# Seven block products for eight in the second feed-forward product of an encoder step, its weight remainders made by accumulating transfers

## The reference

```python
h = _rmsnorm(x, g_mix); p = h @ w_in                  # 1024 -> 7168
x = x + (sigmoid(g_conv)*conv_branch + sigmoid(g_attn)*attention) @ w_out
def _mlp(x, g, w_up, w_down):
    h = _rmsnorm(x, g)
    return jnp.square(jax.nn.relu(h @ w_up)) @ w_down # 1024 -> 4096 -> 1024
x = x + _mlp(x, g_mlp, w_up, w_down)                  # then a final RMSNorm
```

## Time and profile before

| | |
|---|---|
| median of 3 runs | 952.39 us |
| the profiled execution | 951.78 us, of which the traced span is 950.0 us |
| PE busy | 940.7 us, 99% |
| DVE, ACT, POOL busy | 535.8 us, 527.2 us, 257.2 us |
| DMA | 111.37 MB, mean 117 GB/s |

### The profile page before, as it was taken

The page is one execution under the profiler, slowest core; times in us unless marked ns, Lnnn a source line. Parts: engine busy times, 40 slices in busy tenths (PEclk is TensorE's granted clock), DMA queues, the critical chain, the costliest instruction groups (busy, mean ns, idle before and its releaser), DMA issues.

```text
span 950.0 us, 19721 instructions
## 1 busy us (share of the span) xinstructions
PE 940.7 (99%) x7473; PEld 922.4 (97%) x7473; DVE 535.8 (56%) x917; ACT 527.2 (55%) x824; POOL 257.2 (27%) x188
## 2 busy tenths in 40 slices
PE   8999999999999999999999999999999999999997
PEld 8999999999999999999999999999999999999997
DVE  6579999999999999996753332221111122221133
ACT  6788888878787878786733343333111133331153
POOL 5311110101010101012243444445333244454340
PEclk9999999999999999999999999999999999999999
DMA  6777676766767585668132223233323133243102
GB/s 181 163 170 144 154 145 156 133 169 125 176 120 181 112 188 105 148 154 203 45 110 89 83 76 108 87 90 112 89 89 89 47 89 88 88 122 97 45 23 95
DMA packets 189520, 111.37 MB, mean 117 GB/s; under 512 B 35437, under 2 KB 181277, under 8 KB 189482
## 3 DMA queue, kind: packets, MB, share of 16 engines
q1 hardware_dynamic: 176666, 80.28, 30.7%
q0 software_dynamic: 7632, 27.79, 16.1%
q10 hardware_dynamic: 5184, 2.78, 1.1%
HBM read 75.97 MB, written 7.06 MB: 87 GB/s over the span
## 4 chain that ended last, share of the span: by engine, by line
PE 95%; ACT 1%; DMA 1%; POOL 1%; DVE 1%; issue 0%; ACTq 0%; DVEq 0%
PE dense L551 81%; PE z L671 3%; PE dense L846 3%; PE z L635 2%; PE z L705 2%; POOL w_lo L516 1%; PE z L551 1%; DMA w_lo<-w_raw 1%; PE z L639 1%; DMA x_tok<-in_x_sample_dram 1%; PE dense L715 0%; ACT n L957 0%; PE z L838 0%; PE z L629 0%; PE z L691 0%; PE z L710 0%
## 5 line engine op out<-in xcount | busy, mean ns | idle before, releaser
L534 POOL TENSOR_TENSOR w_lo<-w_raw,w_hi 128x1024 fp32r<-128x1024 f32 x80 | 192.3, 2408 | 294.9 <-ACT w_hi L939 294.9
L551 PE MATMUL dense<-r_hi,w_hi 128*128 128x272 f32 (+1 forms) x1264 | 263.5, 291 | 1.2 <-DMA w_lo<-w_raw 0.7
L551 PE MATMUL dense<-r_lo,w_hi 128*128 128x272 f32 (+1 forms) x1264 | 262.7, 289 | 0.0
L551 PE MATMUL dense<-r_hi,w_lo 128*128 128x272 f32 (+1 forms) x1264 | 262.3, 289 | 0.0
L939 ACT ACTIVATE w_hi<-w_raw 128x1024 fp32r<-128x1024 f32 x134 | 140.7, 1052 | 115.4 <-PE dense L551 102.7
L551 PEld LDWEIGHTS dense<-r_hi,w_hi 128*128 128x128 f32 x1264 | 198.2, 188 | 1.6 <-DMA w_lo<-w_raw 0.8
L551 PEld LDWEIGHTS dense<-r_lo,w_hi 128*128 128x128 f32 x1264 | 198.8, 188 | 0.7 <-DVE r_lo L1352 0.6
L551 PEld LDWEIGHTS dense<-r_hi,w_lo 128*128 128x128 f32 x1264 | 199.2, 188 | 0.0
L1371 DVE SCALAR_TENSOR_TENSOR acc<-conv_in,cw_cur,acc 128x574 f32<-128x574 f32 x232 | 172.8, 809 | 0.5
L511 POOL DMA_DIRECT2D w_lo<-w_raw x53 | 45.1, 851 | 361.2 <-ACT w_lo L941 361.2
L551 PE MATMUL dense<-s_hi,w_hi 128*128 128x272 f32 x640 | 132.2, 288 | 0.0
(11 more groups left out here) (258 smaller groups left out, 1287.0 us busy)
## 6 DMA issues: line engine op xcount, KB each, us to landing
w_raw<-in_w_in_dram SPq DMA_DIRECT2D x54, 512.0 KB, 6.0
w_lo<-w_raw POOLq DMA_DIRECT2D x53, 512.0 KB, 5.0
w_raw<-in_w_up_dram SPq DMA_DIRECT2D x32, 512.0 KB, 4.0
w_raw<-in_w_down_dram SPq DMA_DIRECT2D x32, 512.0 KB, 3.5
w_raw<-in_w_pw_dram SPq DMA_DIRECT2D x8, 512.0 KB, 3.6
w_raw<-in_w_out_dram SPq DMA_DIRECT2D x8, 512.0 KB, 3.5
x_tok<-in_x_prompt_dram SPq DMA_DIRECT2D x4, 512.0 KB, 6.1
out_dram<-k_blk SPq DMA_DIRECT2D x32, 64.0 KB, 2.4
```

Source lines behind the costliest of these rows:

```text
L534: pool.tensor_tensor(w_lo[:, n], w_raw[:, n], w_hi[:, n].bitcast(F32), ALU.subtract).then_inc(lo_post, 1)
L551: mm = nc.tensor.matmul(out[:, h, 0:half], w[:, wslot, k, :], m[:, k, c0 + h * half:c0 + (h + 1) * half], start=(k == 0 and n == 0), stop= ...
```

## The change

Three of four rounds of the down product are done as a 2 x 2 block product with seven products for eight (Strassen's method in Winograd's form). A round covers 8 feature blocks. For each of its four pairs of output tiles (`P_`, 12 in all), A is the pair's weights, divided into even and odd output tile and even and odd feature block; B is the activations, divided into even and odd feature block and first and second 272 tokens. PE makes seven products (`SEVEN`), each of 4 blocks x 3 passes = 12 matmuls of 272 columns. DVE adds them to `xT` in nine additions from PSUM (`add_product`).

The forms of A are A11, A12, A22 and four sums S1 to S4, each 128 x 512. DVE makes the four sums (`wsum_pair`, into part of `gate_c`); ACT writes the rounded form into `w_hi` and the rounded negated form into `w_lo`; POOL then issues one accumulating transfer of 256 KB for each form. The forms of B (four quarters, of which three are used as they are, and T1 to T4, DVE's) are made in `up`. The feed-forward part now runs as four rounds of 8 up tiles, each followed by its part of the down product; the fourth is as before.

```diff
+        BY_DMA = ('A11', 'S1', 'A12', 'S2', 'S4', 'S3', 'A22')
+        SEVEN = (("A11", "B11", 0, True), ("S1", "T1", 1, True), ("A12", "B21", 2, True), ("S2", "T2", 0, False),
+                 ("S4", "B22", 3, True), ("S3", "T3", 0, False), ("A22", "T4", 2, True))
+        def quarter(P_, name):
+            slot = 2 * (P_ % 2) + (name[1] == "2")
+            return w_raw[:, slot].rearrange("p (k t) c -> p t k c", t=2)[:, int(name[2]) - 1]
...
# SP
+            def seven_left(P_, b):
+                for name in ("A11", "A12") if b == 0 else ("A22",):
+                    low_made(sync, P_, name)
+                sync.wait_ge(wsum_done, len(SUM_FORMS) * (P_ + 1))
...
+                    for j in range(2):
+                        for n in range(4):
+                            if j == 0:
+                                seven_left(PAIRS * (rr - 1) + 2 + n // 2, n % 2)
...
+                            if p < 2:
+                                sync.wait_ge(lo_post, lows_of_post(g0 + 1, slot))
+                            else:
+                                seven_left(P_ - 2, b)
+                            sync.dma_start(w_raw[:, slot], wdown_v[:, rr, :, 2 * p + b, :]).then_inc(raw_seven[slot], 16)
...
# POOL
+            def seven_low(P_):
+                for name in BY_DMA:
+                    pool.wait_ge(wform_hi, PRODUCTS * P_ + MADE[name])
+                    pool.dma_start(form_place(w_lo, name).bitcast(F32), raw_form(P_, name), accum_op=ALU.add).then_inc(wform_lo[MADE[name] - 1], 16)
...
# PE
+            def seven(rr, p):
...
+                for name, moving, b, begin in SEVEN:
+                    low_made(pe, P_, name)
...
+                    before = {"S2": "x11", "S3": "x12", "A22": "z11"}.get(name)
+                    if before:
+                        pe.wait_ge(product_added, N_ADDED * P_ + ADDED[before])
...
+                    for m in range(PAIRS):
+                        if p == 0 and m == PAIRS - 1:
+                            pe.wait_ge(form_ready, form_count(rr, m, moving))
+                        for j, (w, low) in enumerate(((hi, False), (hi, True), (lo, False))):
+                            mm = nc.tensor.matmul(product_bank(P_, b), w[:, m, :], u_form(moving, m, low), ...)
+                    mm.then_inc(product_done, 1)
...
# ACT: up, and the forms
+                        nc.scalar.activation(u_form("B21", m), halves[0], ACT.Copy).then_inc(form_hi, 1)
+                        nc.scalar.activation(u_form("B22", m), halves[1], ACT.Copy).then_inc(form_hi, 1)
+                        for name in ("T2", "T3", "T4"):
+                            u_sum_high(rr, m, name)
...
+            def seven_free(P_, name):
+                rr, p = divmod(P_, PAIRS)
+                if p == 0:
+                    act.wait_ge(tile_done, FIRST_POST + 4 * (up_group(rr) + 1) + FORM_HOME[name][0] + 1)
+                else:
+                    act.wait_ge(product_done, PRODUCTS * (P_ - 1) + MADE[name])
...
+                    form_high(P_, "A11")
+                    up(g, rr, 5, 1)
+                    form_high(P_, "S1", "A12", "S2")
+                    up(g, rr, 6, 2)
+                    form_high(P_, "S4", "S3")
+                    up(g, rr, 7, 3)
+                    form_high(P_, "A22")
+                    for p in range(1, PAIRS):
+                        form_high(P_ + p, *MADE)
...
# DVE, a later pair of a round
+                    made(P_, "A11")
+                    add_product(P_, "x11")
+                    following("S1", "S2")
...
+                    made(P_, "A12")
+                    add_product(P_, "z11", "x11")
+                    following("S4")
...
+                made(P_, "S2")
+                add_product(P_, "x12")
+                add_product(P_, "y12", "x12")
```

More of the change, by code:

```diff
@@ L284, in build @@
         h2_ready, u32_done, uhi_done, u_ready = (sem(n) for n in ("h2_ready", "u32_done", "uhi_done", "u_ready"))
+        raw_seven = [sem(f"raw_seven{n}") for n in range(4)]
+        wform_hi, wform_lo = sem("wform_hi"), [sem(f"wform_lo{n}") for n in range(PRODUCTS)]
+        wsum_done = sem("wsum_done")
+        usum_done, form_hi, form_ready = sem("usum_done"), sem("form_hi"), sem("form_ready")
+        product_done, product_added = sem("product_done"), sem("product_added")
         fin_done = sem("fin_done")
@@ new lines, in low_made, with form_place @@
+        def low_made(engine, P_, name):
+            engine.wait_ge(wform_lo[MADE[name] - 1], (16 if name in BY_DMA else 1) * (P_ + 1))
+        MADE = {w: n + 1 for n, (w, _, _, _) in enumerate(SEVEN)}
+        ADDED = {"x11": 1, "z11": 2, "x12": 3, "y12": 4, "w12": 5, "x22": 6, "x21": 7, "y22": 8, "z21": 9}
+        N_ADDED = len(ADDED)
+        def form_place(buf, name):
+            slot, h = FORM_HOME[name]
+            return buf[:, slot, h * PAIRS:(h + 1) * PAIRS, :]
+        def quarter(P_, name):
+            slot = 2 * (P_ % 2) + (name[1] == "2")
+            return w_raw[:, slot].rearrange("p (k t) c -> p t k c", t=2)[:, int(name[2]) - 1]
@@ new lines, in _ @@
+            for rr in range(ROUNDS):
+                g0 = up_group(rr)
+                if rr > 0:
+                    pe.wait_ge(product_added, N_ADDED * (PAIRS * rr - 1))
+                with pe.Fori(g0 + 1 if rr == 0 else g0, g0 + 2) as g:
+                    group(g, s_hi, s_lo)
+                if rr < N_SEVEN:
+                    for p in range(PAIRS):
+                        seven(rr, p)
+            pe.wait_ge(product_added, N_ADDED * PAIRS * N_SEVEN)
+            for f in range(4):
+                unit(LAST_GROUP - 1, f, u_hi, u_lo, (u_ready, 1) if f == 0 else None)
+                if f >= 1:
+                    pe.wait_ge(xg_done, f)
+                    back(f - 1, ((0, 0), (1, 1), (2, 2), (3, 3)))
@@ new lines, in _ @@
+            dve.wait_ge(rstd_done, 2)
+            for rr in range(ROUNDS):
+                for f in range(KC):
+                    up(rr, f)
+                    if rr < N_SEVEN and f == 4:
+                        for name in SUM_FORMS:
+                            wsum_pair(PAIRS * rr, name)
+                    if rr < N_SEVEN and f == 5:
+                        wsum_low(PAIRS * rr, "S1")
+                        wsum_low(PAIRS * rr, "S2")
+                if rr < N_SEVEN:
+                    for p in range(PAIRS):
+                        seven_added(PAIRS * rr + p)
```

260 lines of the change are left out of this document (198 added, 62 removed).

## The result

| | before, run beside it | after |
|---|---|---|
| median (four runs each) | 952.28 us (951.65 to 952.46) | 979.54 us (978.49 to 980.45) |
| ratio, 95% interval | | 1.0282 (1.0269 to 1.0294) |
| traced span, mean granted clock | 950.0 us | 977.9 us, 0.990 |

The change costs 27.3 us; 11.2 were forecast. The direction and the bound were right, the size was too small by 16 us and the time lies above the range (948 to 976).

The account below looks back on a forecast made before the run. PE, busy 940.7 of 950.0 us, was taken to bound the kernel before, DMA the products after. Median 952.4 less 18.8 us of matmuls plus 30.0 of PE waits gave 963.6 us; range 948 to 976 for 8 in 10.

Parts of the forecast that it names:

- The gain: Down product's three changed rounds: seven products for eight save 18.8 us if PE never waits.
- The bound: In the products, DMA becomes the bound: 13.4 us of transfers and loads in 10.45 us of PE a pair; chance 0.59.
- 262,144 B take 1.35 us: Price of one sum's accumulating transfer in the products, from a full window at 194 GB/s.
- I take 1.21 and 1.63 us: Raw forms' transfers in 512 B runs: 1.21 times slower, as plain loads are, so 1.63 us each.
- The other waits are covered by this one: In each product round, the start's forms of B and DVE's sums' chain add nothing beyond the 10.0 us DMA wait.
- A22: First pair's last form in each round: lands at 10.0 us, wanted at 8.96, so PE waits 1.0 us.
- the cover of the up tiles: Up tiles' weights load and round during the fourth pair, costing nothing; if that fails, about 2.4 us a round.
- Rival 1: Raw forms' transfers: short runs cost nothing, a round waits 7.2 us, 955.2 us in all; chance 0.15.
- Rival 2: Products' transfers: DMA keeps up at 213 GB/s, 1.23 us a form, a round waits 4.6 us, 947.4 us; chance 0.13.
- point of decision: DMA work in a product round below which the faster rival decides: 38.2 us.
- Rival 3: POOL's issue of raw forms grows with pieces, up to 3.4 us, making POOL the bound: 972 us; chance 0.10.
- Rival 4: PE's clock falls during waits in the products, giving 985 us or more; chance 0.03.

Follow-up runs that it names:

- e2: The changed kernel with each accumulating transfer carrying only one of its form's four blocks, the other low parts left out: 938.4 us.
- e4: The changed kernel with five transfers a pair instead of seven, DVE subtracting the low parts of S1 and S2: 950.8 us.
- e9: The changed kernel with five transfers a pair (low parts of S1 and S2 by DVE) and raw forms read in one long run a partition: 941.6 us.
- e5: The changed kernel with raw forms read in long runs and DVE's additions ahead of the next pair's sums: 964.0 us.
- e3: The changed kernel with DVE's additions put ahead of the next pair's sums, raw forms still in short runs: 975.0 us.
- e1: The changed kernel with up tiles reordered so that each raw form is read as one run of 2 KB a partition: 974.5 us.
- e11: The changed kernel with three transfers a pair, all four sums' low parts by DVE, raw forms read in short runs: 946.2 us.
- e10: The changed kernel with three transfers a pair, all four sums' low parts by DVE, raw forms read in long runs: 942.8 us.
- e6: The changed kernel with five transfers a pair (low parts of S1 and S2 by DVE), long runs and DVE's additions first: 947.6 us.
- e12: e9 with ACT copying the first pair's A22 before it takes up the last up tile: 942.9 us.

## Why the prediction was wrong in its size

- **The gain** (18.8 us) was right: e2 has it, less 1.3 us because a product's matmul takes 0.1257 us and not 0.1244.
- **The bound** was right: DMA share at and above 1, PE at 37.8 of 44.6 us (0.85), idle at all forms of the later pairs, and the loss gone when transfers are taken out (e4, e9).
- **The step that failed** is "262,144 B take 1.35 us" with "I take 1.21 and 1.63 us". The price of a sum came from transfers of 512 KB, whose pieces are 4 KB; the new ones have pieces of 2 KB and 512 B. The packet records show that a piece has a fixed part: in an accumulating transfer a piece of 4 KB, 2 KB and 512 B takes 338, 178 and 65 ns (medians). The last two give about 27.5 ns and 0.0735 ns a byte, which for 4 KB makes 329 ns; the most frequent value there is 328. By windows, a form of 256 KB costs 1.35, 1.52 and 1.94 to 1.99 us. So the ratio of raw forms to the 4 KB pieces is 1.44 to 1.47, and not the loads' 1.21. With both, a round's work is 47.2 and not 41.9 us, its wait 15.3 and not 10.0, and the time 952.4 - 18.8 + 46.0 = 979.6. By this formula 12 x 0.17 x 3 = 6.1 of the 16 us missed come from the sums and 10 x 0.33 x 3 = 9.9 from the raw forms. The runs bear out the second term: the full windows of raw forms agree, and e5 against e3 gives 0.37 us between the two kinds, where 0.28 was forecast and the windows have 0.44. The first rests on one window out of a spread of 1.28 to 1.61 us. PE's balance divides the same 16 us in another way, 7.9 of waits, 5.4 of clock, 1.3 of matmuls and 1.5 outside; the formula leaves the last three out, so part of its agreement is luck. The range had held both ends together at 980 and then cut them off.
- **"The other waits are covered by this one"** was wrong in its mechanism. The load behind A22 was to land 3.5 to 6.0 us later; it took 12.1 us. Its pieces of 512 B go through the same engines as the queued transfers: in the records from 622 to 625 us about 81 transfer pieces of 2 KB and 87 load pieces of 512 B a microsecond, one for one by their numbers. A load that gets a turn for each large piece of another gets few of the bytes, here 44 of some 210 GB/s. DVE's chain then ended at t = 25.5 (PE goes on at 630.28), where 16.5 to 19.0 was forecast; PE was to want it at 19 and, late by then itself, wanted it at 22.5. While the rate binds this costs little on top: with the additions first e3 wins 4.5 us of its 13.1 us of waits, and 1.3 of these 4.5 are clock. It eats the gain when the rate is eased alone (e1: 5.0 of 13.2 us).
- **A22** was right: at 10.5, for 10.0; PE waited 1.7 us for 1.0 in the first round and 1.1 in the others. So was the cover of the up tiles: eight of them take 47.8 us between rounds, 5.97 each.
- **Rival 1**, short runs free, fell. e5 against e3 (11.0 us) and e11 against e10 (3.4 us) show them at 0.37 us a form, or less where the engines have room. The rule of the Trainium skill (DMA: Bandwidth & Descriptors, Why small descriptors are slow (HBM only)), that transfers within SBUF don't suffer from small pieces, does not hold for these accumulating transfers, SBUF on both sides: 132 GB/s in pieces of 512 B, 163 to 205 in pieces of 2 KB.
- **Rival 2** fell: no full window of sums reached 213 GB/s in this kernel (205 at most). Its point of decision, 38.2 us of work, was good: e4, with 38.1, is at 950.8 us, and its 1.6 us under the kernel before are less than the 1.9 that can be told from none.
- **Rival 3** fell: 1.29 us for four times the pieces, not 3.4; ACT is what POOL waits for, and e1 with issues of 0.86 us is still 22 us slower than before.
- **Rival 4** was there in part, and the prediction had put the clock at nothing in its main case. In the rounds the granted clock fell to 0.5 three times, for 3.4, 6.8 and 6.8 us: once 0.4 us after a wait of 3.3 us, twice within waits of 5.2 and 5.5. In 749.4 to 753.4 us 18 matmuls took 0.222 us each for 0.126: 1.7 us lost. All 55 slow matmuls lost 5.4 us. How much of that the kernel's time holds is open, since a PE that is faster there might only wait longer for the transfers. The Trainium skill (TensorE: Matmul & The Clock Gate, HAM oscillation) describes this; the trace agrees in kind, and what it takes here is far from the 33 us of that rival (985 us against the 952 of before).

What stays open. The agreement of 979.6 with 979.5 is closer than the parts deserve: the formula is too long by 2 us a round for e5 and too short by 2.7 for e1 and e6. Late additions, late sums and the clock are not in it, and its price of a sum is one of a wide spread. No run held PE's clock up through its waits, so what the half clock costs in the end was not separated from the waits. In e1, whose matmuls lose as much to it as in after, the missing 8 us go with the late additions (19.9 us for 13.1). The one-for-one turns of loads and transfers are read from packet records and were not tested by a run of their own.

## What to carry to other kernels

Saving matmuls (18.8 us of PE) pays only if what feeds them fits beside them: sum the DMA time of a stretch against PE's time in it, and price each transfer by its pieces, a fixed part and a part by bytes, not by the rate of a transfer with larger pieces. When the sum is over, spread the work: with two of seven low parts on DVE, which had room, and the others read in one run a partition, the same idea is at 941.6 us, 1.15% faster than the kernel it started from. An order that helps under one bound (additions first, -4.5 us) can harm under the next (+6.0 us), so it is to be tried again after each change of the bound.

## What the runs showed of the hardware beyond this

- An accumulating transfer takes about twice as long a piece as a plain one: 338 for 166 ns at 4 KB, 178 for 87 at 2 KB, 65 for 27 at 512 B (medians of the packet records of after).
- A transfer of 512 KB took 12.1 us beside queued transfers, and 3.9 in the median.
- A short wait can cost more than its length: after a wait of 2.2 us inside a busy stretch, e9's next 15 matmuls took 0.225 us each for 0.126, 1.5 us. Not each does: a wait of 2.1 us for A22 was followed by a fall of the clock in e10 and by none in e11, and e12 had none after one of 3.0 us.
